# Hybrid decoder trunk: a recurrent stage whose elementwise work leaves GpSimd

## The reference

```python
xy = h @ w_in + b_in                     # h = rmsnorm(x); w_in: 1024 x 2048
xb, yb = jnp.split(xy, 2, axis=-1)
gate = jax.nn.gelu(yb)
xc = causal_conv4(xb, conv_w) + conv_b   # 4 taps per channel
r = sigmoid(xc @ gate_w[0] + gate_b[0])  # 8 blocks of 128 x 128
i = sigmoid(xc @ gate_w[1] + gate_b[1])
log_a = -8.0 * r * softplus(-lam)
a = exp(log_a)
bx = sqrt(-expm1(2.0 * log_a)) * (i * xc)
hs = scan of h_t = a_t * h_(t-1) + bx_t over the tokens
x = x + (hs * gate) @ w_out
```

## Time and profile before

| | us |
|---|---|
| median of 3 runs | 1179.99 |
| lowest and highest | 1178.47, 1181.94 |
| span of the profiled execution, first to last instruction | 1174.9 |
| PE busy in it | 1108.2 (94%) |
| DVE busy | 653.9 (56%) |
| ACT busy | 480.1 (41%) |
| POOL busy | 202.2 (17%) |

### The profile page before, as it was taken

One profiled execution on the slowest core, in us unless ns is written; L12 is line 12 of the kernel. 1 busy time (PEld: TensorE's weight loads), 2 busy tenths in 40 slices (PEclk: granted clock), 3 DMA queues, 4 the chain that ended last, 5 costly groups with the idle time before them and its releaser, 6 DMA issues.

```text
span 1174.9 us, 13923 instructions
## 1 busy us (share of the span) xinstructions
PE 1108.2 (94%) x4856; PEld 887.3 (76%) x4856; DVE 653.9 (56%) x937; ACT 480.1 (41%) x745; POOL 202.2 (17%) x141
## 2 busy tenths in 40 slices
PE   8889689999999999999998989889999999999995
PEld 5667568888888888888876656668888888888884
DVE  7997985543443433446467787867533433433434
ACT  6448554422322422434335655745422422422342
POOL 4556733000000000012012242223000000000013
PEclk9989899999999999999999999999999999999998
DMA  5112213222223222232311111113222232222322
GB/s 221 54 54 72 81 48 122 90 90 97 101 90 107 89 97 99 89 108 90 108 54 55 54 53 37 36 54 126 90 98 100 90 107 89 95 102 89 107 72 72
DMA packets 30293, 102.42 MB, mean 87 GB/s; under 512 B 3248, under 2 KB 5552, under 8 KB 30128
## 3 DMA queue, kind: packets, MB, share of 16 engines
q1 hardware_dynamic: 29968, 100.74, 24.9%
q10 hardware_dynamic: 288, 1.18, 0.3%
HBM read 99.81 MB, written 2.10 MB: 87 GB/s over the span
## 4 chain that ended last, share of the span: by engine, by line
PE 78%; DVE 15%; ACT 4%; issue 2%; POOL 1%; DMA 0%; DVEq 0%; SPq 0%; ACTq 0%
PE ps L1251 70%; PE ps L1369 4%; DVE gelu L923 2%; DVE prob L1142 1%; ACT prob L705 1%; PE ps L1432 1%; DVE w_lo L822 1%; DVE lru_v L923 1%; DVE prob L1139 1%; DVE lru_v L949 1%; PE ps L1406 1%; DVE lru_r L985 1%; DVE inv_lam L1137 1%; DVE h_lo L827 1%; DVE lru_v L989 1%
## 5 line engine op out<-in xcount | busy, mean ns | idle before, releaser
L1251 PE MATMUL ps<-u_hi,w_hi 128*128 128x512 f32 x696 | 281.7, 405 | 16.9 <-POOL u_lo L409 12.0
L486 ACT ACTIVATE w_hi<-w_raw 128x1024 fp32r<-128x1024 f32 x184 | 193.5, 1052 | 245.8 <-PE ps L1251 196.8
L1251 PE MATMUL ps<-h_hi,w_hi 128*128 128x512 f32 x704 | 282.5, 401 | 3.5 <-DVE h_lo L827 2.2
L1251 PE MATMUL ps<-h_lo,w_hi 128*128 128x512 f32 x704 | 277.8, 395 | 0.0
L1251 PE MATMUL ps<-h_hi,w_lo 128*128 128x512 f32 x704 | 277.8, 395 | 0.0
L1251 PE MATMUL ps<-u_lo,w_hi 128*128 128x512 f32 x696 | 272.8, 392 | 0.0
L1251 PE MATMUL ps<-u_hi,w_lo 128*128 128x512 f32 x696 | 272.8, 392 | 0.0
L822 DVE TENSOR_TENSOR w_lo<-w_raw,w_hi 128x1024 fp32r<-128x1024 f32 x164 | 204.4, 1247 | 17.7 <-ACT w_hi L486 17.6
L1251 PEld LDWEIGHTS ps<-u_hi,w_hi 128*128 128x128 f32 x696 | 131.4, 189 | 52.8 <-issue 11.3
L1251 PEld LDWEIGHTS ps<-h_hi,w_hi 128*128 128x128 f32 x704 | 134.6, 191 | 35.6 <-DVE h_lo L827 4.1
L1251 PEld LDWEIGHTS ps<-h_lo,w_hi 128*128 128x128 f32 x704 | 134.7, 191 | 28.6 <-issue 1.0
(11 more groups left out here) (174 smaller groups left out, 1010.2 us busy)
## 6 DMA issues: line engine op xcount, KB each, us to landing
w_raw<-weights SPq DMA_DIRECT2D x184, 512.0 KB, 3.2
x<-x_t SPq DMA_DIRECT2D x8, 256.0 KB, 5.4
y_t<-att SPq DMA_DIRECT2D x8, 256.0 KB, 2.3
gelu<-gate_weights ACTq DMA_DIRECT2D x1, 1024.0 KB, 5.7
lam_in<-lam_vecs ACTq DMA_DIRECT2D x1, 128.0 KB, 2.0
vec<-vectors SPq DMA_DIRECT2D x1, 64.5 KB, 1.9
```

The costliest lines, as they stand in the source:

```text
L486: nc.scalar.activation(w_hi[:, t % RING, :], w_raw[:, t % RAWS, :], ACT.Copy).then_inc(whi_done, 1)
L1251: ins = nc.tensor.matmul(ps[:, bank, :], w[:, slot, ws], o[:, k, :], start=(k == 0 and n == 0), stop=(k == NCH - 1 and n == 2))
```

## The change

In the recurrent stage, and in the opening before it:

- POOL loses all its work there. The `w_lo` of tiles 4 to 15, the products by the gate and by the root, and `u_lo` go to DVE; one minus the decay goes to ACT (`root`, a Copy with scale -1 and bias 1). POOL keeps some tiny operations on 128 x 8 at the start, which make `conv_c`, the convolution's constant with the bias folded in, and the pads, which hold minus the bias.
- All 8 chunks have padded buffers of their own (`pad`). DVE writes the scaled branch there without the bias, and ACT does the last tap with scale and bias (`tap`) in place of the addition of the bias. DVE does three taps.
- The gate products take the unsplit operands: one F32 matmul each in place of three passes. The gate weights are loaded at the program's start on ACT's queue, ahead of all its work, and not split.
- GELU is one ACT instruction per chunk.
- The sums of squares for the first norm are 8 accumulating F32 matmuls of PE, one behind each step (`first_stats`), and not POOL's additions with one matmul.
- The 16 projection tiles are interleaved (`IN_ORDER`): x0 to x4, then y and x in turn, then y4 to y7; the lists of ACT, DVE and PE are written out to match. Numbers of tiles, their sizes and all later stages stay.

```diff
+
+IN_ORDER = ("x0", "x1", "x2", "x3", "x4", "y0", "x5", "y1", "x6", "y2", "x7", "y3", "y4", "y5", "y6", "y7")
+XT = [IN_ORDER.index(f"x{m}") for m in range(NCH)]
...
         h_lo = sb("h_lo", [P, NCH, S], F32R)
+        early = ExitStack()
+        gw = sb("gw", [P, 2 * NCH * P], F32, early)
+        pad = sb("pad", [P, NCH, PAD + S], F32, early)
...
+            taps = [vec[:, COLS["conv_w"] + j * NCH:COLS["conv_w"] + (j + 1) * NCH] for j in range(CONV_W)]
+            b_x = vec[:, COLS["b_in"]:COLS["b_in"] + NCH]
+            for j in range(PAD):
+                own.step(nc.gpsimd.tensor_scalar(pad[:, :, j:j + 1].rearrange("p m o -> p (m o)"), b_x, -1.0, 0.0, ALU.mult, ALU.add))
+            own.step(nc.gpsimd.tensor_tensor(conv_c[:, :], taps[0], taps[1], ALU.add))
+            for j in range(2, CONV_W):
+                own.wait()
+                own.step(nc.gpsimd.tensor_tensor(conv_c[:, :], conv_c[:, :], taps[j], ALU.add))
+            own.wait()
+            own.step(nc.gpsimd.tensor_tensor(conv_c[:, :], conv_c[:, :], b_x, ALU.mult))
+            own.wait()
+            nc.gpsimd.tensor_tensor(conv_c[:, :], conv_c[:, :],
+                                    vec[:, COLS["conv_b"]:COLS["conv_b"] + NCH],
+                                    ALU.add).then_inc(conv_consts, 1)
...
-            for m in range(NCH):
-                split_lo(m + RING)
-                if m:
-                    gated_input(m - 1)
-            gated_input(NCH - 1)
-
-
...
 
             nc.scalar.preload_act_table_set("natural_log_exp_and_others")
...
+            def first_square(m):
+
+                if m >= 4:
+                    act.wait_ge(stat_mm, m - 3)
+                nc.scalar.activation(work[:, m % 4, :], x[:, m, :], ACT.Square).then_inc(sq_done, 1)
...
-                if m == 4:
-
-                    nc.scalar.dma_start(gw_raw, gate_weights).then_inc(gw_in, 16)
+                if m:
+                    first_square(m - 1)
                 if m == NCH - 2:
                     split_hi(2)
-                square(N_A, m)
+            first_square(NCH - 1)
...
-            nc.scalar.activation(gw_hi, gw_raw, ACT.Copy).then_inc(gwhi_done, 1)
...
+
+            def tap(m):
+
+                act.wait_ge(bank_read, XT[m] + 1)
+                nc.scalar.activation(lru_v[:, m, :], pad[:, m, PAD:], ACT.Identity,
+                                     scale=col("conv_w", PAD * NCH + m),
+                                     bias=conv_c[:, m:m + 1]).then_inc(tap_done, 1)
...
-                nc.scalar.activation(xc_hi[m % 2], xc[m % XC], ACT.Copy).then_inc(xchi_done, 1)
...
+            def tanh(m):
+
+                act.wait_ge(gates_act, m + 1)
+                act.wait_ge(ix_done, m + 1)
+                nc.scalar.activation(lru_v[:, m, :], lru_r[:, m, :], ACT.Tanh,
+                                     scale=small[:, 8, m:m + 1]).then_inc(tanh_done, 1)
...
+                nc.scalar.activation(lru_r[:, m, :], lru_r[:, m, :], ACT.Exp,
+                                     scale=small[:, 9, m:m + 1]).then_inc(lru_exp, 1)
...
+                nc.scalar.activation(lru_v[:, m, :], lru_v[:, m, :], ACT.Sqrt,
+                                     scale=-1.0).then_inc(sqrt_done, 1)
+                nc.scalar.activation(lru_r[:, m, :], lru_r[:, m, :], ACT.Copy, scale=-1.0,
+                                     bias=1.0).then_inc(lru_a, 1)
+
+            def gelu_of(m):
+                act.wait_ge(bank_read, YT[m] + 1)
+                nc.scalar.activation(gelu[:, m, :], gelu[:, m, :], ACT.Gelu_apprx_tanh,
+                                     bias=col("b_in", NCH + m)).then_inc(gelu_done, 1)
...
+            tap(0)
+            split_hi(4)
+            tap(1)
+            sigmoids(0)
+            split_hi(5)
+            tap(2)
+            tanh(0)
+            sigmoids(1)
+            split_hi(6)
+            tap(3)
+            tanh(1)
+            sigmoids(2)
+            split_hi(7)
+            tap(4)
+            tanh(2)
+            sigmoids(3)
+            split_hi(8)
+            tanh(3)
+            for c in range(0, 4):
+                decay_exp(c)
+            tap(5)
+            split_hi(9)
+            for c in range(0, 4):
+                root(c)
+            split_hi(10)
+            sigmoids(4)
+            tap(6)
+            split_hi(11)
+            tanh(4)
+            sigmoids(5)
+            split_hi(12)
+            tanh(5)
+            tap(7)
+            split_hi(13)
...
+            for c in range(4, NCH):
+                decay_exp(c)
+            split_hi(16)
+            for c in range(4, NCH):
+                root(c)
+            split_hi(17)
+            for m in range(0, 6):
+                gelu_of(m)
+            split_hi(18)
+            gated_hi(0)
+            gated_hi(1)
+            gelu_of(6)
+            gated_hi(2)
+            gated_hi(3)
+            gelu_of(7)
+            split_hi(19)
+            for c in range(4, NCH):
+                gated_hi(c)
             nc.scalar.preload_act_table_set("natural_log_exp_and_others")
...
-                t = T_XB + m
+                t = XT[m]
...
-                nc.vector.tensor_tensor(zr[m % 2], ps[:, t % RING, :], rstd[:, :],
+                nc.vector.tensor_tensor(pad[:, m, PAD:], ps[:, t % RING, :], rstd[:, :],
                                         ALU.mult).then_inc(bank_read, 1)
...
+            def y_scaled(m):
+                t = YT[m]
+                dve.wait_ge(tile_done, t + 1)
+                nc.vector.tensor_tensor(gelu[:, m, :], ps[:, t % RING, :], rstd[:, :],
+                                        ALU.mult).then_inc(bank_read, 1)
+
+            def conv(m):
+                dve.wait_ge(tap_done, m + 1)
                 for j in range(PAD - 1, -1, -1):
-                    own.wait()
                     ins = nc.vector.scalar_tensor_tensor(
-                        out=xc[m % XC], in0=pad[:, j:j + S], scalar=col("conv_w", j * NCH + m),
-                        in1=xc[m % XC], op0=ALU.mult, op1=ALU.add)
+                        out=lru_v[:, m, :], in0=pad[:, m, j:j + S], scalar=col("conv_w", j * NCH + m),
+                        in1=lru_v[:, m, :], op0=ALU.mult, op1=ALU.add)
                     if j:
                         own.step(ins)
+                        own.wait()
                     else:
                         ins.then_inc(conv_done, 1)
...
-                nc.vector.tensor_tensor(xc_lo[m % 2], xc[m % XC], xc_hi[m % 2],
-                                        ALU.subtract).then_inc(xclo_done, 1)
...
+            def gated_input(m):
+                dve.wait_ge(gates_act, m + 1)
+                nc.vector.tensor_tensor(lru_x[:, m, :], lru_x[:, m, :], lru_v[:, m, :],
+                                        ALU.mult).then_inc(ix_done, 1)
...
+            decay()
+            norm_newton(N_A)
+            dve.wait_ge(conv_consts, 1)
+            branch(0)
+            branch(1)
+            conv(0)
+            split_lo(4)
...
+            gated_input(2)
+            split_lo(7)
             y_scaled(0)
-            for m in range(NCH):
-                if m < NCH - 1:
-                    gelu_arg(m)
-                if m == NCH - 2:
-                    gelu_arg(m + 1)
-                for n in Y_AT.get(m, ()):
-                    y_scaled(n)
-                for c in DECAY_AT.get(m, ()):
-
-                    dve.wait_ge(lru_exp, c + 1)
-                    own.step(nc.vector.scalar_tensor_tensor(
-                        out=lru_r[:, c, :], in0=lru_r[:, c, :], scalar=1.0, in1=lru_v[:, c, :],
-                        op0=ALU.add, op1=ALU.mult))
-                    own.wait()
-                    nc.vector.scalar_tensor_tensor(
-                        out=lru_v[:, c, :], in0=lru_r[:, c, :], scalar=-2.0, in1=lru_r[:, c, :],
-                        op0=ALU.add, op1=ALU.mult).then_inc(lru_q, 1)
-                for c in SCAN_AT.get(m, ()):
-                    recurrence(c)
-                    if c == 0:
-
-                        dve.wait_ge(wlo_done, T_OUT)
-                        split_lo(T_OUT)
-                if m == 3:
-
-                    split_lo(T_OUT + 1)
-                    split_lo(T_OUT + 2)
-                gelu_gate(m)
-                for c in GATED_AT.get(m, ()):
-                    gated(c)
-
-            dve.wait_ge(olo_done, O_Y + NCH - 1)
-            dve.wait_ge(ohi_done, O_Y + NCH)
-            nc.vector.tensor_tensor(u_lo[:, NCH - 1, :], lru_v[:, NCH - 1, :], u_hi[:, NCH - 1, :],
-                                    ALU.subtract).then_inc(olo_done, 1)
+            conv(4)
+            gated_input(3)
+            split_lo(8)
+            decayed(0)
+            branch(5)
+            split_lo(9)
+            for c in range(1, 4):
+                decayed(c)
+            y_scaled(1)
+            conv(5)
+            split_lo(10)
+            scaled_input(0)
+            recurrence(0)
+            branch(6)
+            split_lo(11)
+            scaled_input(1)
```

(66 more changed lines are left out.)

255 lines of the change are left out of this document (76 added, 179 removed).

## The result

| | before | after |
|---|---|---|
| median of 4 runs each, us | 1179.23 (1178.46 to 1181.94) | 1158.72 (1157.5 to 1158.89) |
| ratio, 95% interval | 1 | 0.9818 (0.9807 to 0.983) |
| profiled span, us | 1174.9 | 1156.8 |
| opening, to the first scaled bank | 29.5 | 36.3 |
| recurrent stage, to the last `u_lo` | 134.5 | 107.9 |

The account below looks back on a forecast made before the run. The prediction took VectorE, slowed by GpSimd, to bound the recurrent stage. Stage -27.8 us and opening +4.0 gave -23.8, so 1180.0 became 1156 us, range 1147 to 1168.

Parts of the forecast that it names:

- That VectorE bounds the stage, by GpSimd's doing: Recurrent stage: VectorE sets its 134.5 us because VectorE and GpSimd slow each other; new stage 106.7, 27.8 us less.
- What goes is the slowing: VectorE's list in the recurrent stage: instruction count hardly moves, the slowing by GpSimd goes; quiet rows sum to 88.5 us.
- The quiet prices: VectorE rows without GpSimd beside them: three taps 2.33 us, plain ones 0.61, `w_lo` 1.14, scan 1.55.
- The waits: VectorE's waits in the recurrent stage: 5.6 us for TensorE, 7.6 for ScalarE, 1.0 first tap; 14.2, plus 3.0 for the clock.
- PE itself waits some 6 us: Before the last gate products, `gates(7)`: TensorE idles some 6 us for the eighth convolution, y4's tile queued behind.
- PE's list is shorter, so it doesn't set the end: Recurrent stage: TensorE's tiles and gate products sum to 90.6 us, less than VectorE's 106.7.
- The opening: Before the first scaled bank: `rstd` 4.0 us later, from the gate weights' load and TensorE's statistics; bounds 1.4 and 5.7.
- The table load: ScalarE in the recurrent stage: a load costs 1.30 us, its successor starts at its end; the skill gives about 2.66.
- Rival B: Recurrent stage: TensorE and VectorE wait by turns, six more falls of the clock cost 10 us, 1166; chance 0.19.
- C: Opening and recurrent stage: loads don't delay tile 0, clock falls hide under VectorE's work, 1150; chance 0.15.
- D: Recurrent stage: VectorE's slow rows are the chain's own nature, not GpSimd's doing; 13 us slower, 1193; chance 0.03.

Follow-up runs that it names:

- e2: Changed kernel with the `w_lo` of tiles 4 to 15 back on GpSimd; 1157.94 us, ratio 0.9806.
- e6: Changed kernel plus 24 idle GpSimd additions of 128x512, two behind each high part of tiles 4 to 15; 1167.72 us, ratio 0.9896.
- e7: Changed kernel plus 24 idle GpSimd copies of 128x512, two behind each high part of tiles 4 to 15; 1161.18 us, ratio 0.9841.
- e11: e5 with the gate products of chunk 0 put behind tile 3 in place of tile 2; 1144.8 us, ratio 0.9706.
- e1: Changed kernel with the gate weights' load issued behind the sixth chunk of the opening, no longer first; 1154.3 us, ratio 0.9777.
- e3: Changed kernel without the second gate product of each chunk, both sigmoids reading the first one's bank; 1153.67 us, ratio 0.9763.
- e4: Changed kernel with ScalarE's `w_hi` of tiles 9, 11 and 13 ahead of the tap that stood before each; 1153.46 us, ratio 0.9765.
- e5: Changed kernel with the edits of e1 and e4 together; 1150.39 us, ratio 0.9753.
- e8: Changed kernel with the first normalization's sum of squares back on GpSimd in place of eight F32 products; 1155.82 us, ratio 0.9798.
- e9: Kernel before with only the gate products changed, each one F32 product of unsplit operands; 1174.82 us, ratio 0.9963.
- e10: Changed kernel with one of the three VectorE taps of each convolution left out; 1152.95 us, ratio 0.9773.

## Why the prediction was right, step by step

- **That VectorE bounds the stage, by GpSimd's doing.** That GpSimd slows VectorE's rows is shown (e2, e6, e7), and without it the convolutions are quiet; no run took GpSimd's work out of the kernel before, so its share there is inferred. "What goes is the slowing" tells half: VectorE's busy time fell by 35.8 us. At the prices of the forecast the 32 operations that left VectorE are worth about 19.5, the 35 that came cost 27.7 (12 x 1.14 + 23 x 0.61), and up to 6.2 left with the decay's constants. By that estimate 38 to 44 us of slowing went, and the moved work took 27.7 of it back. The quiet prices held: taps 2.33, plain ones 0.60 to 0.61, `w_lo` 1.14. Only the scan was too dear, 1.55 where it is 1.14. The scans of the earlier trace rows weren't quiet (GpSimd's `u_lo` ran from 152.87 to 154.14, beside the first of them), so the list is 3.3 us shorter: 8 x 1.14 in place of 8 x 1.55. 88.5 was forecast, VectorE was busy 84.41.
- **The waits.** 14.2 was forecast, with 3.0 for the clock. For TensorE it is 11.6 (6.4 + 5.2) against 5.6 + 3.0; for ScalarE 9.9 (7.6, 1.4, 0.5 and 0.4) against 8.6, the tap included. The places were right but for their size: 3.19, 2.02, 2.02 and 4.35 at chunk 3, chunk 4, y0 and y4, where I had 0.5, 1.6, 1.5 and 2.0; the high parts of tiles 9, 11 and 13 made 1.83 each (1.6 to 1.7 forecast), the first decay 1.42 (1.5). "PE itself waits some 6 us" before `gates(7)` was wrong: it waited 2.03. The two falls of the clock came where they were forecast, at the first gates and at the last.
- **The step that failed: "PE's list is shorter, so it doesn't set the end".** The two sums, 90.6 and 106.7, were compared side by side over the whole stage, but the lists stand in a row: VectorE's last 28.8 us start only when TensorE has made y4's bank, and TensorE, with no gap from 42 to 103.4 us, needs 70.2 up to there even in e11, where nothing stops it. 70.2 + 28.8 is e11's whole stage of 98.9. The missing 3 us of waits (11.6 for TensorE against 5.6 + 3.0) are VectorE waiting for this list. The too dear scan hid it: 4.1 us less of busy time against 4.3 more of waits in all (3.0 for TensorE, 1.3 for ScalarE) and 1.0 more of small gaps, so the stage came out as 107.9 against 106.7 forecast, -26.6 instead of -27.8. That the sum is this near is luck.
- **The opening.** +4.0 forecast, +6.7 measured. The delay of the first tile (2.4 forecast, 2.7 measured) and the step (2.26 forecast, 2.24 measured) were right. What was missing is a fall of the clock in the opening, which stood only as the upper bound of 5.7: behind the 2.19 us that TensorE waits for the late first tile its products up to the last statistics take 2.5 us more than in e1. The load that came first thus had two prices, and e1 takes both away.
- **The table load.** 1.30 forecast, and ScalarE's timeline shows 1.28 with its successor 0.02 behind:

```profile
68.38 1.28 ACT L514 ACT_TABLE_LOAD   x1
69.68 2.57 ACT L514 ACTIVATE lru_r<-lru_r,small 128x512 f32<-128x512 f32 x4
```

  The Trainium skill (ScalarE: Activation LUTs, "What ACT_TABLE_LOAD costs") would have made the wait behind it 1.4 us longer; the trace doesn't agree with it in this kernel, neither here nor at the switch to the GELU (load at 123.96, successor at 125.25).
- **Rival B** (by turns, 1166) was half true: the two engines do take turns, but the clock fell at two places of the stage, not at eight. **C** (no delay of the loads, and falls that hide) is refuted by the first `w_hi` at 8.11 and by e1, whose stage is 3.3 shorter without the two falls, **D** (slow rows by nature) by eight convolutions of 2.33 and by e6. The output projection and the rest moved by 0.9 and 0.8, which I had at nothing.
- On the spans -18.1 was measured against -23.8: +2.7 from the opening, +1.2 from the stage, +1.7 from behind it. The medians differ by 20.5, so the spans make the miss look larger by 2.4.

## What to carry to other kernels

Don't compare the lists of two engines as sums over a stage: find where one has to wait for the other, cut there, and add the pieces that stand in a row. An edit pays only in a piece that its engine sets, or by a pause that it takes away. A large load that is needed late must not be issued first, for the pause it makes on TensorE is paid again in clock. And moving work from GpSimd to VectorE is no gain by itself when it costs VectorE as much as the slowing did; what pays is work that goes away or to an engine with room.

## What the runs showed of the hardware

- GpSimd delays VectorE's SBUF-to-SBUF rows, and the delay goes by the GpSimd instruction: 0.40 us for a copy, 0.83 for an addition (a product of 0.69 us takes 1.09 and 1.52), and about 2.0 for a subtraction of 128x1024 (three taps of 2.33 take 4.28 and 4.32 in e2). In the rows read here one VectorE row pays it, not every row beside GpSimd. In e6 the `w_lo` at 91.59 started just before the pair of additions, lies beside them and takes the 1.23 that it takes alone; the next two products pay 0.84 each, one for each addition:

```profile
91.64 3.53 POOL L360 TENSOR_TENSOR bias<-bias 128x512 f32<-128x512 f32 x2 [4.34 <-ACT w_hi L437]
```
```profile
91.59 1.23 DVE L787 TENSOR_TENSOR w_lo<-w_raw,w_hi 128x1024 fp32r<-128x1024 f32 x1 [1.83 <-ACT w_hi L437]
92.73 1.53 DVE L908 TENSOR_TENSOR lru_x<-lru_x,lru_v 128x512 f32<-128x512 f32 x1
```

- VectorE's read of a bank isn't slowed: with the additions, the row at 98.98 lies wholly beside GpSimd and takes the 0.68 that it takes alone. The addition went on during it, for the `w_lo` behind it pays only 0.24 (the two timelines of e6):

```profile
98.71 3.24 POOL L360 TENSOR_TENSOR bias<-bias 128x512 f32<-128x512 f32 x2 [3.54 <-ACT w_hi L437]
```
```profile
98.98 0.68 DVE L875 TENSOR_TENSOR gelu<-ps,rstd 128x512 f32<-128x512 f32 x1
99.58 1.46 DVE L787 TENSOR_TENSOR w_lo<-w_raw,w_hi 128x1024 fp32r<-128x1024 f32 x1
```

  The Trainium skill (GPSIMD Engine Reference, "Specifications") names VectorE's instructions with two SBUF inputs among those that contend with GpSimd; a bank read has one, and the 0.68 us agree.
- The clock falls behind a pause of TensorE, but not always behind the same one. Behind pauses of 2.34 to 2.36 us before the first gates it fell in the profiles of both runs of the changed kernel, e3, e4 and e5, and stayed up in e1; behind 2.01 to 2.03 before the last gates it fell in both of the changed kernel and in e8, and stayed up in e1. In e9 it stayed up behind 1.94 and 2.19. Behind the pauses before gates of 0.76 to 1.73 (e2, e6, e10) it stayed up, behind those of 2.57 to 7.0 (e2, e3, e6, e7, e8, e9) it fell. A fall costs 1.6 us of the stage (8.11 against 6.53 between two convolutions). It may be why e1's runs lie between 1149.34 and 1155.27; that was not tested.
- An F32 product of 128x128 by 128x512 costs TensorE 0.88 us of its pace ((7.20 - 5.44) / 2), where three passes in the split form cost 0.68 at the pitch of 0.227.
